# Rotary tables, one query turn, two query roots and three table loads moved in the second attention

## The reference

```
h = rmsnorm(x, norm_mix);  proj = h @ gqa_w_in        # q 8x128, k 2x128, v 2x128, q_mem 4x128
q = rope(rmsnorm(q, q_norm));  k = rope(rmsnorm(k, k_norm))     # 2-D rotary, rows and columns
mix = softmax(q k^T * 128**-0.5) v                    # 8 query heads share 2 key heads
mem_n = rmsnorm(mem, mem_norm);  mk, mv = split(mem_n @ w_mem_kv)
mem_out = softmax(rmsnorm(q_mem) rmsnorm(mk)^T * 128**-0.5) mv  # 4 heads, 256 memory rows
x = x + concat(mix, mem_out) @ w_out
```

## Time and profile before

| what | us |
|---|---|
| three runs | 2534.4, 2534.82, 2535.25 |
| median | 2534.82 |
| the profiled execution: its time | 2534.8 |
| its span, first to last instruction | 2533.0 |
| TensorE busy | 2499.9 |
| POOL, ACT, DVE busy | 1399.3, 1080.7, 1012.7 |

### The profile page before, as it was taken

How to read it: one execution, slowest core, us unless ns; L and a number is a source line. 1 busy time by engine, 2 the same in 40 slices (tenths; PEclk the granted TensorE clock), 3 DMA queues, 4 the chain that set the end, 5 groups by cost and what they waited for, 6 DMA issues and landing times.

```text
span 2533.0 us, 36304 instructions
## 1 busy us (share of the span) xinstructions
PE 2499.9 (99%) x12584; PEld 2015.5 (80%) x12584; DVE 1012.7 (40%) x2186; ACT 1080.7 (43%) x1833; POOL 1399.3 (55%) x1084
## 2 busy tenths in 40 slices
PE   9999999999999999999999999999999999999999
PEld 7878888888877888888866588888888757888887
DVE  7567542125576652114676522111025562211100
ACT  6336552235437453225456533333134463333321
POOL 6425755566624765567744535656456263565653
PEclk9999999999999999999999999999999999999999
DMA  5312113224212212333320123333333102233322
GB/s 195 100 51 84 44 50 97 95 84 143 92 50 84 68 35 84 96 96 117 117 75 26 34 75 92 99 99 92 99 119 106 50 26 72 93 93 99 99 93 74
DMA packets 62366, 215.11 MB, mean 85 GB/s; under 512 B 7312, under 2 KB 10512, under 8 KB 61840
## 3 DMA queue, kind: packets, MB, share of 16 engines
q1 hardware_dynamic: 62224, 213.28, 27.1%
HBM read 211.16 MB, written 2.10 MB: 84 GB/s over the span
## 4 chain that ended last, share of the span: by engine, by line
PE 78%; issue 10%; POOL 8%; DVE 2%; ACT 1%; DMA 0%; SPq 0%; POOLq 0%; ACTq 0%; DVEq 0%
PE bank L853 20%; PE bank L854 20%; PE bank L855 20%; POOL wl L2455 6%; PE pair L1591 2%; PE pair L853 2%; PE pair L855 2%; PE pair L854 2%; PE bank L1646 1%; PE bank L1620 1%; PE bank L1192 1%; PE pair L1429 1%; PE pair L1205 1%; PE bank L1163 1%; PE bank L1143 0%
## 5 line engine op out<-in xcount | busy, mean ns | idle before, releaser
L2455 POOL TENSOR_TENSOR wl<-raw,wh 128x512 fp32r<-128x512 f32 x750 | 1004.2, 1362 | 913.0 <-ACT wh L2406 286.7
L853 PE MATMUL bank<-hh,wh 128*128 128x512 f32 x1600 | 632.6, 395 | 1.0 <-ACT rv L1862 0.9
L855 PE MATMUL bank<-hh,wl 128*128 128x512 f32 x1600 | 623.4, 390 | 0.0
L854 PE MATMUL bank<-hl,wh 128*128 128x512 f32 x1600 | 622.9, 389 | 0.0
L853 PEld LDWEIGHTS bank<-hh,wh 128*128 128x128 f32 x1600 | 300.6, 188 | 63.9 <-ACT rv L1862 2.7
L855 PEld LDWEIGHTS bank<-hh,wl 128*128 128x128 f32 x1600 | 300.3, 188 | 63.3
L854 PEld LDWEIGHTS bank<-hl,wh 128*128 128x128 f32 x1600 | 300.7, 188 | 59.5 <-issue 0.5
L2406 ACT CAST wh<-raw 128x1024 fp32r<-128x1024 f32 x120 | 125.6, 1048 | 254.0 <-PE pair L855 140.2
L1828 ACT CAST wh<-raw 128x1024 fp32r<-128x1024 f32 x104 | 109.2, 1051 | 122.3 <-PE bank L855 96.7
L853 PE MATMUL bank<-wh,hh 128*128 128x512 f32 (+2 forms) x352 | 139.1, 395 | 1.5 <-issue 0.7
L2087 ACT CAST wh<-raw 128x1024 fp32r<-128x1024 f32 x84 | 86.9, 1050 | 122.8 <-PE bank L855 103.3
(11 more groups left out here) (471 smaller groups left out, 4671.7 us busy)
## 6 DMA issues: line engine op xcount, KB each, us to landing
raw<-stream SPq DMA_DIRECT2D x384, 512.0 KB, 3.6
mraw<-memin SPq DMA_DIRECT2D x3, 1024.0 KB, 5.6
par<-params SPq DMA_DIRECT2D x2, 1124.5 KB, 8.8
out<-xT SPq DMA_DIRECT2D x8, 256.0 KB, 2.0
con<-consts SPq DMA_DIRECT2D x1, 1540.0 KB, 14.8
xT<-xin SPq DMA_DIRECT2D x2, 512.0 KB, 4.5
xT<-xin SPq DMA_DIRECT2D x1, 1024.0 KB, 8.4
con<-consts SPq DMA_DIRECT2D x1, 512.0 KB, 3.1
```

Source lines behind the costliest of these rows:

```text
L853: mm(o, ah, bh, start=start, stop=False)
L854: mm(o, ah, bl, start=False, stop=False)
L855: return mm(o, al, bh, start=False, stop=stop)
L2455: m = TT(wl[slot][:, c], raw[slot][:, c], wh[slot][:, c].bitcast(F32), ALU.subtract)
```

## The change

VectorE makes the rotary tables of this layer after the roots of the memory, not before; TensorE waits for them (own semaphore, 8) before it turns `mk`, since the tables are read from the bank into which it turns. The turn of tile 1 of `qA` goes to bank 6, and the turns of tiles 0 to 2 each wait for one eviction fewer. The root of `qA` is taken in step 10 of phase 0, that of `qB` in step 5 of phase 1 (they stood together in step 16 of phase 0), with their sums and reciprocals moved to match. After the root of `kv` and after each of these two stands a one-column Exp (`load_exp`, written to `warm`), which makes the table load happen there. Two casts for `qB` go into steps 1 and 2, each behind an Exp of the softmax.

```diff
-LATE_FEATURES = ((None, (12, 14)), ((10, 10), (18, 18)))
+LATE_FEATURES = ((None, (12, 14)), ((12, 10), (18, 18)))
+TABLES_OWN = 8
...
+                    if (i, name, x) == (1, "mk", 0):
+                        pe.wait_ge(t["own"].sem, t["own"].at(TABLES_OWN))
...
+                        if (i, phase) == (1, 0):
+                            pe.wait_ge(t["feat"].sem, t["feat"].at(len(done) - (x < 3)))
+                            turn_one(name, x, bk[6] if x == 1 else bk[7])
+                            return
...
+                def load_exp():
+
+                    A(warm[:, :], eps_b[:, 0:1], ACT.Exp)
+
...
                     take_root("kv")
+                    load_exp()
                     cast("qA", [1])
                     take(lambda name, x: squares(name, 16, x), "qA", "kv")
-                    cast("qA", [2, 3])
...
                         if phase == 0:
+                            if step in (1, 2):
+                                cast("qA", [step + 1])
                             if 5 <= step < 9:
-                                feature("qA", step - 5, bk[7])
+                                feature("qA", step - 5, bk[6] if step == 6 else bk[7])
                             if step % 4 == 0 and 4 <= step <= 16:
                                 squares("qB", 32, step // 4 - 1)
-                            if step == 16:
+                            if step == 10:
                                 take_root("qA")
-                                take_root("qB")
+                                load_exp()
                         elif step in QB_TURNS:
                             feature("qB", QB_TURNS.index(step), bk[6])
+                        elif step == 5:
+                            take_root("qB")
+                            load_exp()
...
-                tables()
+                if i == 0:
+                    tables()
                 memory_moments()
...
                         finish(name)
+                    tables()
+                    assert own.n == TABLES_OWN
...
                         if phase:
+                            if step == 1:
+                                dve.wait_ge(t["evac"].sem, t["evac"].at(evac_at(i, "qB", NT - 1)))
+                                square_sums("qB", 32)
                             if step == 2:
                                 own.end()
+                            if step == 6:
+                                finish("qB")
                             return
...
-                        if step == 16:
-                            dve.wait_ge(t["evac"].sem, t["evac"].at(evac_at(i, "qB", NT - 1)))
-                            count["root"] += 1
-                            square_sums("qB", 32)
-                            count["root"] -= 1
-                        if step == 18:
+                        if step == 10:
                             finish("qA")
-                            finish("qB")
```

More of the change, by code:

```diff
@@ L625, in build @@
     spare = sb("spare", [P, 1])
+    warm = sb("warm", [P, 1])
     mixg = sb("mixg", [P, KD], at=small_at)
```

## The result

| | before | after |
|---|---|---|
| median us | 2534.94 (2534.40 to 2535.79, 20 runs) | 2539.77 (2534.80 to 2543.07, 20 runs) |
| the profiled execution | 2534.8, span 2533.0 | 2541.22, span 2539.4 |

The ratio is 1.0018, with a 95% interval of 1.0012 to 1.0025. The median is 3.8 us above the forecast of 2536.0 and 1.2 us above the upper end of the range. The two kernels differ in another way too: the runs of before lie within 1.4 us, those of after within 8.3, and the fastest of these is as fast as before.

What follows compares the result with a forecast made beforehand. TensorE, busy 99% of the span, was taken to bound the kernel. The terms -0.6 + 0.9 - 1.3 + 0.7 + 1.5 = +1.2 us, added to 2534.8, gave 2536.0, with a range from 2532.8 to 2538.6.

Steps and rivals of the forecast that it cites:

- Where TensorE's time can be won or lost: Whole kernel: TensorE is busy 99%, so only its idle time can be won, about 5.2 us of waits in second attention.
- The sum: Second attention, all five terms: -0.6 + 0.9 - 1.3 + 0.7 + 1.5 = +1.2 us, giving 2536.0.
- The forecast's own last step: What would show it: among other signs, turn of block 4 in phase 1 waits some 3 us for ScalarE's copies, not 0.71.
- The tables behind the memory roots: Turn of `mk`: with tables moved behind the roots, TensorE's whole wait for GpSimd's scaling goes, -0.6 us.
- its other bound, +1.8: Turn of `mk`: VectorE gets through only at the end of GpSimd's run, tables come 3.8 later, TensorE turns at 1927.9.
- locked out: Rival at the memory root: VectorE waits for GpSimd's run to end, +1.8 in place of -0.6, 2538.4; chance 0.15.
- Its deeper form, 2539.6: Locked out also at block 0's scaling until 1990.0, scores of block 4 2.1 later, sum +4.8; within the 0.15 chance.
- The first softmax block: Steps 1 to 4, phase 0: Exp waits go, but late casts make TensorE wait for GpSimd's low halves, +0.9 us.
- The third turn: Third turn of `qA`: with bank 6 for the second turn, its 1.27 us wait for an eviction goes, -1.3.
- The root of `qA`: Step 10, phase 0: root and loads take 3.0 us, delaying block 10's Exp and the scores of block 12, +0.7.
- the root of `qB`: Where phases meet: some 0.6 won at first turn of phase 1, then step 5's root delays block 4's turn, +1.5.
- dearer switches: Rival at the new root places: each root pair costs another 2 x 1.4 us beyond its loads, 2541.6; chance 0.03.

Runs made afterwards that it cites:

- the kernel with the roots alone: The kernel before with only the roots of `qA` (step 10, phase 0) and `qB` (step 5, phase 1) taken apart, one-column Exp behind each: 2538.24 us, ratio 1.0013.

## Why the prediction was wrong

*Where TensorE's time can be won or lost.* Right: every step of the lag lies at a place that the prediction named, and nothing is given back behind this attention. What it missed is that TensorE's idle time is not all that can be lost: behind its two long waits the clock was halved, 1.6 and 1.7 us, 3.3 of the 6.4. The sum had no term for the clock, that is, it put it at nothing without a reason. The forecast's own last step should have raised the question: it named a wait "some 3 us" at the turn of block 4, where the longest of this attention was 1.3. The rest, 3.1 us, is idle time, where the forecast had 1.2 (the busy times of the windows give 3.6 for it, 6.8 to 10.4).

*The tables behind the memory roots: -0.6 taken, +1.9 measured.* This is the step that failed, and its other bound, +1.8, was the right one. The failing sentence is "a like instruction at 1987.15 took 0.83 and got through between two of GpSimd's; I take -0.6". Of the two rows, the one at 1920.00 was the very instruction that moved, and it was held; the one at 1987.15 was another. In all six profiles that have the tables behind and more than one number a row, the first of these instructions was held 7.0 us, past the ends of five of GpSimd's instructions. By the rule of the Trainium skill (SBUF — State Buffer, Who interferes with whom: the pair is held for one whole instruction) it would have got in within 1.3 us. The 0.71 and 1.34 of the kernel with the roots alone agree with it, the 7.0 do not, and the measurement decides. The rival "locked out" priced the place rightly (2538.4), with a chance of 0.15. Its deeper form, 2539.6, lies next to the measured median by luck: it wants the scaling of block 0 held up until GpSimd's run ends, and in the trace of after that instruction took 0.70 us at 1989.18, beside the run from 1988.44.

*The first softmax block: +0.9, measured +0.7.* Right, with both waits for the low halves (0.89, 0.83) and the addition on top of GpSimd's run. The second of them is the binding of GpSimd that was there before.

*The third turn: -1.3, measured -1.5.* Right; the wait is gone.

*The root of `qA`: +0.7, measured +0.8, and the root of `qB`: +1.5, measured +1.3.* Right in place, mechanism and size, but for a wait of 0.5 for GpSimd behind the first turn of phase 1, which the forecast doesn't have and which went too. The load of 1.28, the Sqrt of 0.22, the load and an Exp of 0.20 make the 3.0 us of the forecast, and the one-column Exp cost the value taken. The switch costs no more than its load: "dearer switches" is out. The Trainium skill's drain (ScalarE: Activation LUTs, What ACT_TABLE_LOAD costs) is not to be seen here, the next instruction starts 0.01 to 0.02 us behind the load.

*The sum.* With +1.9 for -0.6 it would have been +3.7, 2538.5; with the half clock twice, 3.3, it is 7.0, against 6.4 in the profile. The half clock and the lockout do not come in each execution, which fits the spread of over 8 us in the runs of after: its fastest, 2534.80, would fit one with neither (6.4 less 3.3 and less 2.5 or more is under 0.6), though no profile shows it; its mean clock, 0.999, leaves room for a stretch like the free one of the first attention.

Open: what lets VectorE in at one end of a GpSimd instruction and not at five others, and what makes the half clock follow one wait of 2.6 us and not another of 2.85, or the same waits of the first attention in four traces of fourteen. That the long waits bring it in this attention rests on two pairs of kernels (the root of `qB` moved from step 5, and from step 11, to step 10: wait and half clock went together) and on the counts of the clock; it holds for how often it comes, not for each execution.

## What to carry to other kernels

Where a row shows an instruction held up, price its move by that row, not by a milder one of the same kind, and look at what other work stands beside it at the new place. A wait of TensorE that grows from 1 to 3 us can cost half as much again through its clock, and here a wait of 0.2 and one of 0.6 in its place did not. Put a one-off piece of ScalarE (a root with its table loads, 3.0 us) where the next consumer is furthest, found in the timeline and not by its step number: for `qB` steps 5, 11 and 10 cost about 2.4, 2.0 and 1.1 us of TensorE's time, before the clock; for `qA` the place behind the Exp of step 9 cost nothing, where behind the `mPT` it cost 0.8.

## What the hardware showed that was not expected

VectorE, beside a back-to-back run of GpSimd's 128x512 instructions (one every 1.25 us), was held to the end of the run, 7.0 us in six traces that begin at 1916 and 3.2 us in two that begin at 1920, with instructions of 128x4 and 128x2, as TENSOR_SCALAR and as SCALAR_TENSOR_TENSOR, while 128x1 ones took 0.21 us each, eight in 1.06, in the same run. In one execution 128x4 ones that began at 1919.81 got in after 0.71 and 1.34 us.

In the second attention TensorE's clock was granted at half for 3.4 us (once 6.8) at waits of 1.9 us and of 2.5 to 3.2 us, in ten kernels: from 0.9 us before the wait's end to 1.3 behind it, with a loss of 1.4 to 1.7 us (2.9 the once). It stayed at the 2.4 GHz level behind a wait of 2.85, and behind all of the 1.3 to 1.4 us waits there. In the first attention, behind waits of 1.65 and 0.78 us, it was halved for 3.4 us in four traces of fourteen, at no cost.
